# Mixing the next head's projections into the decode-state steps of an mLSTM layer

## The reference, cut to what matters

```python
proj = xn @ w_in
q, k, v, o, gi, gf = jnp.split(proj, MLSTM_SPLITS, axis=-1)
...
num = (jnp.einsum('bhls,bshe->blhe', scores, vc)
       + jnp.einsum('blhd,bhde->blhe', qc, C) * w_inter.transpose(0, 2, 1)[..., None])
...
C_new = carry_w[..., None, None] * C + jnp.einsum('bhs,bshd,bshe->bhde', decay, kc, vc)
...
hf = h * lax.rsqrt(jnp.mean(h * h, axis=-1, keepdims=True) + EPS) \
    * head_g.astype(jnp.float32).reshape(H, MLSTM_DV)
gate = jax.nn.sigmoid(o.astype(jnp.float32)).reshape(B, T, H, MLSTM_DV)
out = (hf * gate).reshape(B, T, H * MLSTM_DV).astype(xn.dtype) @ w_out
```

## Time and profile before

| | |
|---|---|
| median of 6 runs | 4806.66 us (4796.29 to 4885.36) |
| the profiled execution's own time | 4833.5 us |
| its span on the slowest core | 4831.9 us |
| TensorE / VectorE / ScalarE / POOL busy in the span | 77% / 36% / 23% / 10% |
| chain that ended last, by engine | PE 64%, DMA 14%, DVE 9%, ACT 6%, issue 4% |
| the four heads on this core | about 413 to 1648 us of the span |
| TensorE busy from 413 to 1648 us, and its granted clock | 783.7 of 1235 us, 0.68 |
| a state load (sc), from issue to landing | 4.1 us median, 64 of 512 KB |
| a state store (o_cs), from issue to landing | 4.2 us median, 64 of 512 KB |

### The profile page before, as it was taken

The page is one execution under the profiler, slowest core; times in us unless marked ns, Lnnn a source line. Parts: engine busy times, 40 slices in busy tenths (PEclk is TensorE's granted clock), DMA queues, the critical chain, the costliest instruction groups (busy, mean ns, idle before and its releaser), DMA issues.

```text
span 4831.9 us, 55113 instructions; the slowest of 8 cores (4767.9 to 4831.9 us)
## 1 busy us (share of the span) xinstructions
PE 3697.3 (77%) x19156; PEld 1836.7 (38%) x19156; DVE 1747.2 (36%) x2890; ACT 1112.0 (23%) x2190; POOL 461.1 (10%) x350
## 2 busy tenths in 40 slices
PE   5398739458384492899999999466673999999992
PEld 4255314124141142444444444233232444444441
DVE  6200430423314207244334443726114443333335
ACT  5211231321323214211221112410223111222211
POOL 0000010010100104000000000400012000000003
PEclk6699757567586695999999999677785999999996
DMA  4244052061340626554345531450437444344424
GB/s 152 27 61 64 17 151 46 27 152 18 114 83 13 158 40 179 80 70 60 53 62 70 70 53 28 168 88 13 65 83 170 71 68 60 60 63 66 70 44 165
DMA packets 256676, 374.61 MB, mean 78 GB/s; under 512 B 11318, under 2 KB 218422, under 8 KB 244022
## 3 DMA queue, kind: packets, MB, share of 16 engines
q0 software_dynamic: 221760, 232.93, 30.9%
q1 hardware_dynamic: 34646, 138.16, 8.8%
HBM read 495.51 MB, written 75.83 MB: 118 GB/s over the span
## 4 chain that ended last, share of the span: by engine, by line
PE 64%; DMA 14%; DVE 9%; ACT 6%; issue 4%; POOL 2%; DVEq 0%; ACTq 0%; SPq 0%; POOLq 0%
PE bank L432 22%; PE bank L416 20%; PE bank L444 16%; PE bank L396 6%; DVE ACC L687 3%; DMA o_cs<-ACC 2%; DMA ACC<-sc 2%; DMA WB<-w_up 1%; DMA WB<-w_in 1%; POOL R L366 1%; DVE ACC L867 1%; DMA R<-hscr 1%; DVE ACC L707 1%; DMA R<-xin 1%; ACT R L287 1%
## 5 line engine op out<-in xcount | busy, mean ns | idle before, releaser
L439 DVE TENSOR_TENSOR ACC<-ACC,bank 128x512 f32<-128x512 f32 x1140 | 782.4, 687 | 1190.3 <-PE bank L432 1162.7
L432 PE MATMUL bank<-R 128*128 128x512 bf16 (+1 forms) x4864 | 1071.4, 379 | 24.0 <-ACT R L420 24.0
L416 PE MATMUL bank<-XNT,WB 128*128 128x512 bf16 (+1 forms) x6144 | 1021.4, 329 | 80.9 <-DMA WB<-w_up 80.9
L416 PEld LDWEIGHTS bank<-XNT,WB 128*128 128x128 bf16 x6144 | 530.4, 98 | 577.9 <-issue 93.1
L432 PEld LDWEIGHTS bank<-R 128*128 128x128 bf16 (+1 forms) x4864 | 461.3, 97 | 620.1 <-issue 86.7
L418 ACT ACTIVATE R<-bank 128x512 bf16<-128x512 f32 (+1 forms) x384 | 190.0, 495 | 1696.2 <-PE bank L416 1681.5
L444 PE MATMUL bank<-WB,XNT 128*128 128x512 bf16 (+3 forms) x1920 | 398.1, 376 | 0.0
L444 PE MATMUL bank<-XNT,WB 128*128 128x512 bf16 (+3 forms) x1632 | 302.4, 352 | 82.5 <-DMA WB<-w_in 54.5
L444 PE MATMUL bank<-ACC 128*128 128x512 bf16 (+5 forms) x832 | 180.5, 364 | 200.8 <-DVE hsm L640 127.5
L426 POOL DMA_DIRECT2D R<-w_down x128 | 95.3, 747 | 1886.9 <-PE bank L432 1886.9
L444 PEld LDWEIGHTS bank<-WB,XNT 128*128 128x128 bf16 (+1 forms) x1920 | 197.6, 104 | 198.4 <-issue 143.5
(11 more groups left out here) (146 smaller groups left out, 2598.6 us busy)
## 6 DMA issues: line engine op xcount, KB each, us to landing
WB<-w_up POOLq DMA_DIRECT2D x32, 2048.0 KB, 23.7
R<-w_down POOLq DMA_DIRECT2D x128, 512.0 KB, 7.6
ACC<-sc SPq DMA_DIRECT2D x64, 512.0 KB, 4.1
o_cs<-ACC POOLq DMA_DIRECT2D x64, 512.0 KB, 4.2
WB<-w_in POOLq DMA_DIRECT2D x12, 2048.0 KB, 15.7
hscr<-R SPq DMA_DIRECT2D x15, 1024.0 KB, 6.1
R<-xin SPq DMA_DIRECT2D x14, 1024.0 KB, 6.1
R<-hscr SPq DMA_DIRECT2D x14, 1024.0 KB, 6.6
```

Source lines behind the costliest of these rows:

```text
L416: S.op("pe", (lambda kc=kc, b=b, c0=c0, ncol=ncol, fc=fc, wu=wu: lambda e: e.matmul(banks[b][:, :ncol], lhsT=wu[:, kc, fc * 128:(fc + 1) * ...
L432: S.op("pe", (lambda kc=kc, b=b, col0=col0, n=n, wdv=wdv: lambda e: e.matmul(banks[b][:n, :], lhsT=hid[:, kc, col0:col0 + n], rhs=wdv[:, k ...
L439: S.op("dve", (lambda b=b, a=a, n=n: lambda e: e.tensor_tensor(out=a, in0=a, in1=banks[b][:n, :], op=ALU.add))(), reads=["pb%d" % b, "acc% ...
```

## The change

The body of the projection stage becomes a list of 46 closures, `proj_steps(h)`: four weight loads and 42 groups of 16 matmuls, each with its way out of PSUM. Head 0's list runs by itself, as before. In each head's decode stage the list of the next head is dealt out between the sixteen decode steps, two or three closures behind each; head 3 has nothing to mix in. During the mix the projections take their banks from 0, 2 and 4 only, since the others are in use by the decode steps.

So that the next head's projections may overwrite k, v and o, decode works on copies of tile 8 (k8s, v8s, og8s, made by ScalarE); to make room for them Cqb has one buffer instead of two and etmp is bf16. The transposes of the nine other tiles (`hgt_tiles`) move ahead of decode, tile 8's follows its head_out. The gate is one Sigmoid on ScalarE, straight into og, instead of Exp, add and reciprocal.

```diff
+        bank_pool = [list(range(8))]
...
-        CqbL = [carve(512, BF16).rearrange("p (c e) -> p c e", c=2) for _ in range(2)]
+        CqbL = [carve(512, BF16).rearrange("p (c e) -> p c e", c=2) for _ in range(1)]
+        k8s = carve(128, BF16)
+        v8s = carve(257, BF16)
...
+        def proj_steps(h):
+            steps = []
+            holder = {}
+
+            def ld(key, col, ncol):
+                def f():
+                    holder[key] = load_w(w_in0[:, col:col + ncol], 16, ncol)
+                return f
...
+            steps.append(ld("o", 4096 + 512 * h, 512))
+            for t in range(10):
+                def f(t=t):
+                    wo, wok = holder["o"]
+                    col0, n = TILES[t]
+                    b = nbank()
+                    for kc in range(16):
+                        mm(banks[b][:n, :], XNT[:, kc, col0:col0 + n], wo[:, kc, :], kc == 0, kc == 15, ["xnT", wok], ["pb%d" % b])
+                    S.op("act", lambda e: e.activation(out=og[:n, t, :], in_=banks[b][:n, :], func=AF.Sigmoid), reads=["pb%d" % b], writes=["og%d" % t])
+                steps.append(f)
+            return steps
...
-                S.op("act", (lambda b=b, n=n: lambda e: e.activation(out=etmp[:n], in_=banks[b][:n, :], func=AF.Exp, scale=-1.0))(), reads=["pb%d" % b], writes=["etmp"])
-                S.op("dve", (lambda n=n: lambda e: e.tensor_scalar(out=etmp[:n], in0=etmp[:n], scalar1=1.0, scalar2=None, op0=ALU.add))(), reads=["etmp"], writes=["etmp"])
-                S.op("dve", (lambda n=n, t=t: lambda e: e.reciprocal(out=og[:n, t, :], in_=etmp[:n]))(), reads=["etmp"], writes=["og%d" % t])
...
+        for st_ in proj_steps(0):
+            st_()
+        for h in range(4):
...
+            hgt_tiles(h, [0, 1, 2, 3, 4, 5, 6, 7, 9])
...
+            S.op("act", lambda e: e.activation(out=k8s, in_=ktm[:, 8, :], func=AF.Copy), reads=["ktm8"], writes=["k8s"])
+            S.op("act", lambda e: e.activation(out=v8s[:, 0:513], in_=vdtm[:, 8, 0:513], func=AF.Copy), reads=["vdtm8"], writes=["v8s"])
+            S.op("act", lambda e: e.activation(out=og8s, in_=og[:, 8, :], func=AF.Copy), reads=["og8"], writes=["og8s"])
...
+            qsteps = [(lambda q=q: qstep(q)) for q in range(16)]
+            psteps = proj_steps(h + 1) if h < 3 else []
+            bank_pool[0] = [0, 2, 4]
+            np_, nq_ = len(psteps), len(qsteps)
+            pi = 0
+            for qi in range(nq_):
+                qsteps[qi]()
+                tgt = (np_ * (qi + 1)) // nq_
+                while pi < tgt:
+                    psteps[pi]()
+                    pi += 1
...
+            head_out(h, 8, 128, bA, bD, floortm[:, 8, h:h + 1], gate=og8s, gkey="og8s")
+            hgt_tiles(h, [8], src8=og8s)
```

More of the change, by code:

```diff
@@ L235, in build_nc @@
         bank_excl = set()
+        bank_pool = [list(range(8))]
         def nbank():
[L238 to L242, removed]
+            pool_ = bank_pool[0]
+            i = pool_[bank_ctr[0] % len(pool_)]
+            bank_ctr[0] += 1
+            return i
         wb_ctr = [0]
@@ L630, in build_nc, with head_out @@
         hctr = [0]
-        def head_out(h, t, L, bA, bD, floor_ap):
+        def head_out(h, t, L, bA, bD, floor_ap, gate=None, gkey=None):
             p = hctr[0] % 2
@@ L648, in head_out @@
             S.op("act", lambda e: e.activation(out=hrow[:L], in_=hrow[:L], func=AF.Copy, scale=rsh[:L]), reads=[hk, "rsh" + sx], writes=[hk])
-            S.op("pool", lambda e: e.tensor_tensor(out=og[:L, t, :], in0=hrow[:L], in1=og[:L, t, :], op=ALU.mult),
-                 reads=[hk, "og%d" % t], writes=["og%d" % t])
-        for h in range(4):
+            g_ = og[:L, t, :] if gate is None else gate[:L]
+            gk_ = ("og%d" % t) if gkey is None else gkey
+            S.op("pool", lambda e: e.tensor_tensor(out=g_, in0=hrow[:L], in1=g_, op=ALU.mult),
+                 reads=[hk, gk_], writes=[gk_])
@@ new lines, in proj_steps, with f @@
+                        steps.append(f)
+            steps.append(ld("v", 2048 + 512 * h, 512))
+            for t in range(10):
+                def f(t=t):
+                    wv, wvk = holder["v"]
+                    col0, n = TILES[t]
+                    b = nbank()
+                    for kc in range(16):
+                        mm(banks[b][:n, :], XNT[:, kc, col0:col0 + n], wv[:, kc, :], kc == 0, kc == 15, ["xnT", wvk], ["pb%d" % b])
+                    S.op("act", lambda e: e.activation(out=vdtm[:n, t, 0:512], in_=banks[b][:n, :], func=AF.Copy, scale=dectm[:n, t, h:h + 1]),
+                         reads=["pb%d" % b, "dectm"], writes=["vdtm%d" % t])
+                    S.op("dve", lambda e: e.tensor_copy(out=vdtm[:n, t, 512:513], in_=dectm[:n, t, h:h + 1]), reads=["dectm"], writes=["vdtm%d" % t])
+                steps.append(f)
@@ L764, in build_nc @@
[L764 to L776, removed]
-                        S.op("act", (lambda h=h, c=c, col0_=col0_, n=n, ptb=ptb: lambda e: e.activation(out=HGT[:, 4 * h + c, col0_:col0_ + n], in_=ptb[:, c, :n], func=AF.Copy, scale=hgfm[:, 4 * h + c:4 * h + c + 1]))(),
-                             reads=["pb%d" % b, "hgfm"], writes=["hgT_%d_%d_%d" % (h, c, ti)])
@@ new lines, in qstep @@
+                    load_cq(q + NCQ, h)
+            qsteps = [(lambda q=q: qstep(q)) for q in range(16)]
[9 more added lines that the diff above has]
+                    pi += 1
+            while pi < np_:
+                psteps[pi]()
+                pi += 1
```

81 lines of the change are left out of this document (42 added, 39 removed).

## The result

| | before | after |
|---|---|---|
| median of all runs shown beside each other | 4811.48 us (20 runs) | 4890.89 us (10 runs) |
| ratio after to before, 95% interval | | 1.0091 [1.0054, 1.0128] |
| the profiled execution's own time | 4833.5 us | 4841.46 us |
| its span on the slowest core | 4831.9 us | 4839.8 us |
| TensorE / VectorE / ScalarE / POOL busy | 77% / 36% / 23% / 10% | 74% / 33% / 23% / 10% |

Some executions of either kernel ran several per cent longer with one die at a lower clock; the ratio leaves them out, the medians don't, so the ratio is the result. On the 4806.66 us of the prediction it makes 1.0091 x 4806.66 = 4850 us: inside the range of 4755 to 4875, slower by 0.9%, 36 us above the 4814 that was forecast.

What follows compares the result with a forecast made beforehand. The layer was taken as a row of stages, some TensorE's, some state traffic's, with decode leaving TensorE mostly idle. Terms summed to +32.3 or -18.5 us by clock; the middle, +7 on 4806.66, gave 4814 us, range 4755 to 4875.

Steps and rivals of the forecast that it cites:

- seam: The stretch L to M between two heads of the mLSTM layer; three of them, 257.9, 260.2 and 240.2 us before.
- (a): From the last prompt chunk's end to the next head's first projection step, including the Q load: 29.5 us.
- (c): Fifteen more decode steps, each with matmuls and a 2.1 us wait on Cqb: 49.5 us, or 46.5 at the higher clock.
- (d): Late K, V and O weight loads: stalls of 33.5 us plus 4.8 of restarts, 38.3; 40.8 at the higher clock.
- (b): The next head's projection matmuls, the same as before: 145.8 us at the lower clock or 120.9 at the higher.
- (e): End of the stretch: last eviction, tile 8's head_out, transposes, one Sigmoid/Ln table load, way to the next chunk: 11.1 us.
- L to M: Last prompt chunk's eight matmuls' end (L) to next head's first-chunk twelve-matmul group (M): forecast 274.2 us, 248.8 at higher clock.
- -18.5: Forecast change of the whole kernel in us if the higher clock holds throughout; +32.3 with each stretch's clock as before.
- The rival of a lower clock throughout: All three mixed stages run at the lower clock of head 1's projections: +57.7 us, 4864; chance 0.15.
- head 0's -8: Head 0's projections lose VectorE's backlog, 11.1 us before, of which some 3 stay: -8 us.
- head 3's +1.4: Head 3's decode, with nothing to mix in, starts later but waited for o_np anyway: +1.4 us.
- The rival of late loads: V and O land in 23.7 us like w_up, instead of 17.2: 13 us more between heads, 4853; chance 0.15.

Runs made afterwards that it cites:

- no mixing: Changed kernel with the dealing switched off, so sixteen decode steps run first and then all projections of the next head: 0.9935 of the kernel before.
- the gate alone: Kernel before with only the gate changed, to one Sigmoid in place of Exp, add and reciprocal: 0.9902 of the kernel before.

## Why the prediction was right in kind and short in size

The first seam against the forecast at the higher clock, which is the clock it got (a slot of 48 matmuls of 512 columns without a wait ahead takes 10.62 us at 842.49, so 3.5 a step):

| part of the seam | forecast, us | measured, us |
|---|---|---|
| (a) L to the first projection | 29.5 | 29.1 (608.0 to 637.10) |
| (c) fifteen waits on Cqb | 31.5 (15 x 2.1) | 28.1 |
| (d) waits on K, V, O | 36.0 | 40.0 |
| (b), (c), (d) matmuls with restarts | 140.7 (120.9 + 15.0 + 4.8) | 147.9 (216.0 from 637.10 to 853.11, less the two above) |
| (e) end | 11.1 | 11.9 (853.11 to 864.96) |
| L to M | 248.8 | 257.0 |

In the other seams the waits on K, V and O are 48.5 and 45.5. The first seam is 8.2 us longer than forecast: 4.0 of waits on loads and 7.2 of slower matmuls, less 3.0 in the other rows.

- **Right:** (a), (c) and (e) to within 4 us each. Step 0 starts at L + 13.2 (621.25), 13.0 forecast. The places were right too: all three loads late by POOL's order, Cqb late by ScalarE's order, the gate's backlog gone (M stands 4.2 us behind the projections in head 0, 11.1 before).
- **The clock** was left open and went to the higher end, so that end's -18.5 applies where core 0 of before ran lower. The rival of a lower clock throughout did not come: in none of the nine profiles taken after the prediction did head 0's projections, from 440 to 535 us, show anything but 1.00, on any core, and neither did head 1's where they run as a block (no mixing, the gate alone). The Trainium skill's peak-current limit (TensorE: Matmul & The Clock Gate, Part 1), 13/16, would fit that 0.80, but all eight cores run these projections in all ten profiles, and only one die in one of them showed it.
- **Wrong in size, step (d), the loads:** for the traffic beside a load the forecast added 0 to 3.0 us, the middle 1.5, by what one other megabyte had cost. V and O landed in 15.8 to 21.5 us, not 15.7 to 18.7, and K in 13.2 to 14.7, not 9.2 to 12.2. With the state bytes taken out K falls to 9.2 to 10.0, V and O to 13.8 to 14.9, and the waits to 31.1 to 32.6. At the lone prices the forecast's own sum gives 31.5 (36.0 less three times 1.5), so the place of the loads was priced right and the surcharge for the traffic too low: 2.8 to 5.7 us a load instead of 1.5. One reason shows in the windows: beside V ran the state of two decode steps, some 2 MB and not one. Beside O ran one, and it still took 15.8 to 20.0; why that varies so, no run tells.
- **Wrong in size, the slower matmuls behind stalls:** step (d) charged 1.6 us for each of three stalls, 4.8, and step (c) nothing for the fifteen short stops. The same 800 matmuls took 149.9 us in the changed kernel, 142.3 without the three late loads, 142.0 without the wait for Q as well, and 137.2 with the stops at Cqb gone too. So the three stalls cost 7.5 and the fifteen stops 4.9.
- **What that makes:** at the higher clock the forecast seams were 5.1, 0.6 and 4.3 above those of before on core 5. Measured they are 13.3, 12.6 and 18.0 above. With head 0's -8 and head 3's +1.4 the forecast at that clock was +3.4, or 4810; the 34 us between the two sums of seams make it 4844, against 4850. (By the means over the cores, above, the seams lost some 47 more than forecast, and head 0 gained 14 and not 8: its backlog was priced at the lower clock.) The rival of late loads, "13 more a seam: 4853", names the mechanism and the size that came true better than the forecast's own middle; its price was taken from w_up's 23.7 us, where no load here was that slow, and a part of what came true was the slower matmuls. That the two sizes agree is chance.
- **The table load** (e): paid, and at two places. The loads of ScalarE's tables on core 0, by line (709 is the Sigmoid, 650 the Ln):

```profile
L709 ACT ACT_TABLE_LOAD x4 | 5.1, 1283 | 67.0 <-PE bank L445 67.0
L650 ACT ACT_TABLE_LOAD x4 | 5.1, 1283 | 0.3
```

One for each head at either line, so Sigmoid and Ln share no set, as the Trainium skill has it (ScalarE: Activation LUTs, the section on table sets). The second stands before Ln in (e), as charged; the first stands before the first gate eviction and delays the Cqb behind it, so that the wait at 814.74 is 3.15 us and not 1.9.

## What to carry to other kernels

Before work is dealt into a stage, look where its weight loads land in the issuing engine's list: a load that was a prefetch in one block becomes a stall when it moves next to its first user, and here three such stalls (40 to 49 us a seam), fifteen copies queued behind evictions (28) and the slower matmuls behind both (12) cost more than the 75 us stage that the mixing hid. Issue loads where their buffer comes free: with that alone mixing pays (0.979, where the Sigmoid gate without mixing has 0.990). Then write the next step's small preparations ahead of the big group that fills its slot; with both, and Q's load ahead of the chunks, it is 0.949. Price a load at the traffic that runs for as long as it does, not at its lone time plus a constant.

## What the runs showed of the hardware

- A 2 MB weight block landed in 13.8 to 14.9 us with almost no state traffic and in 15.8 to 21.5 with it, although the DMA engines' mean busy share over the mixed stage was only 0.41. While V loaded it read 1.05 with the traffic and 0.97 without: a low mean share does not mean that a single transfer is undisturbed.
- Stalls cost TensorE more than their own length: the same 800 matmuls were busy 149.9 us at a mean granted clock of 0.84 with waits for four weight blocks and fifteen copies between them, 142.3 at 0.92 with Q's wait and the copies', 142.0 at 0.97 with the copies' alone and 137.2 at 0.98 with neither.
- Head 0's projections were granted 0.78 to 0.92 on the four cores of one die in the profiled execution of the kernel before, and 1.00 on every core in all nine later profiles, whatever the kernel; why, no run here tells.
